# Second FFN input product in two passes over the features, and two of its conditioning units folded there

## The chip, the cores and the metric

The kernel runs on one core of one Trainium2 chip. The metric is the device time in microseconds (us) of one execution, from loading the inputs in HBM to having the output there.

## The reference, cut to what matters

A trunk of two layers over 256 tokens and 2048 features, in float32. Layer 0 mixes by pooling, layer 1 by an HGRN2 recurrence; each is followed by a SwiGLU FFN with 5632 hidden features. Six vectors for each layer (shift, scale and gate of the mixer and of the FFN) come from a conditioning vector.

```python
cond = jax.nn.silu(c)
for layer in range(DEPTH):
    mod = cond @ w_ada[layer] + b_ada[layer]            # 2048 -> 6 * 2048
    sh_m, sc_m, g_m, sh_f, sc_f, g_f = jnp.split(mod[:, None, :], N_MOD, axis=-1)
    h = rms_norm(x, norm_mix_gain[layer]) * (1.0 + sc_m) + sh_m
    y = pool_mixer(...) if layer == 0 else hgrn2_mixer(h, w_in, w_out, ...)
    x = x + g_m * y
    h = rms_norm(x, norm_ffn_gain[layer]) * (1.0 + sc_f) + sh_f
    a, b = jnp.split(h @ w_ffn_in[layer], 2, axis=-1)   # 2048 -> 2 * 5632
    x = x + g_f * ((jax.nn.silu(a) * b) @ w_ffn_out[layer])
return rms_norm(x, final_gain)
```

## The kernel before

**Products.** Every weight matrix is cut into chunks of 512 output columns, and a chunk into steps of 128 input features. A step is six matmuls on TensorE: for each of the two blocks of 128 tokens, high part by high part, high part by low part of the weight, low part of the feature by high part of the weight (L472 to L474), all added up in one of two PSUM buffers `prod`. A chunk with the whole 2048 features has 16 steps. There are 1392 steps in all, numbered through by the counter `step` that each engine keeps for itself; `START` gives the first step of each chunk. The stages, with the name of their first step: pooling (16 steps), first FFN input product (A0, 352 steps), first FFN output product (OUT0, 176), HGRN input product and recurrence (H0, 256), HGRN output product (W0, 64), second FFN input product (IN1, 352), second FFN output product (OUT1, 176). "H+75" below is the 75th step after H0.

**Weights.** Two steps are a pair. SyncE (SP) loads a pair to `raw`, ScalarE rounds it to `w_hi` (`hi`, L759), VectorE takes the rest to `w_lo` (`lo`, L1053), TensorE waits for `lo_ready` at every even step. There are four buffers (`SPL`), and ScalarE waits for `w_used` before it takes one again, so ScalarE and VectorE can be at most six steps ahead of TensorE.

**One order for each engine.** Each engine runs its instructions in the order in which they are written. The work between the products is hung by hand onto step numbers: `recurrence` on each engine does a piece of the HGRN recurrence at given steps after H0, once for each of four head groups of 64 steps. In a group TensorE turns forget and query values at 24 and 34, computes self scores at 37 and 38, eight levels of scores at 40, 45, ... 75 (in the last group at 40, 43, 46, 52, 55, 61, 64, 70, with turns of outputs between), and the output at 79 (74 in the last). VectorE does its part of a level in halves of a tile: exponents (L1394, L1395), decayed keys and queries (L1408, L1409), masked scores (L1429, L1436), five steps later in its own count (`LD`), since it is ahead.

**Conditioning units.** `mod` is computed in 24 units: one of the six vectors of a layer, one half of 1024 of its features. A unit is 16 tiles of `w_ada` of 128x1024. VectorE folds a tile into `acc` by one multiply-add (`fold`, L1088; the first tile of a unit by a multiply, L1085), then adds the bias by two instructions (L1097). `BEHIND` lists the units behind the head with the first and last step of their folds, which `due` spreads evenly. Three steps (`SUM`) behind the last, TensorE sums over partitions (`reduce_unit`): 16 small matmuls for shifts and scales (L516), four matmuls for gates (L537). ScalarE takes the result 8 steps later (`take_unit`). There is one `acc`: the first fold of a unit (L1085) waits for the sum of the unit before it. SP loads the tiles by the same step numbers into four buffers.

**First FFN input product.** For 9 of its 11 pairs of chunks (gate and value), `NA`, it runs in two passes over the features: first all 18 chunks over features 0 to 1023 (8 steps each), whose results ScalarE copies to `part_gate` and `part_value` in SBUF, then all over features 1024 to 2047; VectorE adds the stored halves (L1308, L1313), ScalarE applies SiLU in SBUF (L929). The last two pairs have 16 steps a chunk. Features 1024 to 2047 are normalised 118 steps after A0 (`FEATURES_B`), so their shift and scale units are folded inside the stage.

**Second FFN input product.** All 22 chunks have 16 steps over all features. The features are made by `features` at its start: groups 0 and 1 of 512 features ahead of the first matmuls, group 2 and 3 at steps 4 and 8. All four shift and scale units of this FFN, and the two gate units of HGRN, are folded between H+20 and W+32.

Of the kernel before, what the change touches and what calls it, by code (L numbers as in the profile page):

```python
# [14 lines left out]
CH = 512  # L15
# [24 lines left out]
def build(nc, x, c, norm_mix_gain, norm_ffn_gain, w_ada, b_ada, pool_w, pool_scale, hgrn_w_in,  # L40
# [38 lines left out]
    C_A = NCH  # L79
    C_B = C_A + 2 * NA  # L80
    C_OUT0 = C_B + 2 * NF
    C_H = C_OUT0 + NCH
    C_WOUT = C_H + 4 * NCH
    C_IN1 = C_WOUT + NCH
    C_OUT1 = C_IN1 + 2 * NF
# [7 lines left out]
    A0, B0, H0, W0, IN1, OUT1 = (START[n] for n in (C_A, C_B, C_H, C_WOUT, C_IN1, C_OUT1))  # L93
    OUT0 = START[C_OUT0]
    FEATURES_B = A0 + 118
# [33 lines left out]
    with ctx:  # L129
# [180 lines left out]
        def _(sp):  # L310
# [65 lines left out]
            for part in range(2):  # L376
                for j in range(NA):
                    for o in range(2):
                        load_chunk(w_ffn_in[0], o * F + j * CH, part * HALF, HALF, 0 if part or j or o else AHEAD)
            for j in range(NA, NF):  # L380
                for o in range(2):
                    load_chunk(w_ffn_in[0], o * F + j * CH, 0, KD)
# [15 lines left out]
            for j in range(NF):  # L398
                for o in range(2):
                    load_chunk(w_ffn_in[1], o * F + j * CH, 0, KD)  # L400
# [44 lines left out]
        def _(pe):  # L445
# [155 lines left out]
            def first_half(s):  # L601
                if s == 0:
                    turn_normalised()
                if s % 2 == 0:
                    t.tick("h")
                    pe.wait_ge(h_ready, t.get("h"))

            def second_features(_):
                if t.get("step") - 1 in (FEATURES_B + 2, FEATURES_B + 10):
                    turn_normalised()  # L610

            for c2 in range(2 * NA):
                h_product(second_features, None if c2 else first_half)

            def second_half(s):
                if s % 2 == 0:
                    t.tick("h")
                    pe.wait_ge(h_ready, t.get("h"))

            for j in range(NF):  # L620
                def turn_before(s):
                    if s == TURN:
                        if j <= NA:
                            pe.wait_ge(hidden_ready, j)
                            turn_tok()
                        else:
                            turn_hidden(C_B + 2 * j - 1)
                h_product(turn_before if j else None, None if j else second_half, HALF if j < NA else 0)
                h_product(None, None, HALF if j < NA else 0)
# [111 lines left out]
            for j in range(NF):  # L741
                def turn_in1(k):
                    if k == TURN:
                        turn_hidden(C_IN1 + 2 * j - 1)
                h_product(turn_in1 if j else None, None if j else features)
                h_product()
# [3 lines left out]
        def _(act):  # L750
# [137 lines left out]
            def first_half(k):  # L888
                if k == 0:
                    act.wait_ge(gain_ready, 3)  # L890
                    modulate(gain, mod[:, 1, 0:KD], 0)
                    modulate(gain, mod[:, 1, 0:KD], 1)

            def second_features():
                if t.get("step") == FEATURES_B + 8:
                    act.wait_ge(gain_ready, 4)
                    modulate(gain, mod[:, 1, 0:KD], 2)
                if t.get("step") == FEATURES_B + 16:
                    modulate(gain, mod[:, 1, 0:KD], 3)

            def part_of(chunk_at):
                j, o = (chunk_at - C_A) // 2, chunk_at % 2
                return (part_value if o else part_gate)[:, j]

            for c2 in range(2 * NA):
                def in_a(k):
                    if c2 == 0:
                        first_half(k)
                    second_features()
                    if c2 and k == EVAC:  # L910
                        take(C_A + c2 - 1, part_of(C_A + c2 - 1), ACT.Copy)
                chunk(in_a, AHEAD if c2 == 0 else 0)

# [5 lines left out]
            for j in range(NF):  # L919
                def in_gate(k):  # L920
                    if j == 0 and k == EVAC:
                        take(C_B - 1, part_of(C_B - 1), ACT.Copy)

                def in_value(k):
                    if j and k in (HID - HALF, HID - HALF + 1):
                        take_hidden(j - 1, k - HID + HALF)
                    if j < NA and k == EVAC:
                        evacuated(act, C_B + 2 * j)
                        act.activation(tok[:, :, :], tok[:, :, :], ACT.Silu).then_inc(silu_ready, 1)  # L929
                    if j >= NA and k == EVAC:  # L930
                        take(C_B + 2 * j, tok[:, :, :], ACT.Silu)
                chunk(in_gate)
                chunk(in_value)
# [97 lines left out]
            for j in range(NF):  # L1031
                def in_gate(k):
                    if j == 0:
                        features(k, gain, mod[:, 1, 0:KD], 6)
                    if j and k in (HID, HID + 1):
                        take_hidden(j - 1, k - HID)

                def in_value(k):
                    if k == EVAC:
                        take(C_IN1 + 2 * j, tok[:, :, :], ACT.Silu)  # L1040
                chunk(in_gate, 0 if j else AHEAD)
                chunk(in_value)
# [3 lines left out]
        def _(dve):  # L1046
# [238 lines left out]
            def in_a(_):  # L1285
                g = t.get("step")
                if g == FEATURES_B:
                    gains_of(C_GFFN, 1, HALF, HALF, UNIT[(0, SC_F, 1)])
                    normalise(2)
                if g == FEATURES_B + 8:  # L1290
                    normalise(3, 1)
                    split_feat(2)
                if g == FEATURES_B + 16:
                    split_feat(3)

            for c2 in range(2 * NA):
                def first_half(k):
                    if k == 0:
                        normalise(1, 1)
                        split_feat(0)  # L1300
                        split_feat(1)
                chunk(in_a, 0 if c2 else AHEAD, None if c2 else first_half)

            def add_gate(j):
                multiplied(dve, C_B + 2 * j)
                if j:
                    dve.wait_ge(small_full[1], t.get("small1"))
                dve.tensor_tensor(tok[:, :, :], prod[0][:, :, :], part_gate[:, j], ALU.add).then_inc(prod_free[0], 1)  # L1308

            def add_value(j):  # L1310
                multiplied(dve, C_B + 2 * j + 1)
                pv = part_value[:, j]
                dve.tensor_tensor(pv, prod[1][:, :, :], pv, ALU.add).then_inc(prod_free[1], 1)  # L1313
                dve.wait_ge(silu_ready, j + 1)
                evacuated(dve, C_B + 2 * j + 1)
                dve.tensor_tensor(tok[:, :, :], tok[:, :, :], pv, ALU.mult).then_inc(hidden_ready, 1)

# [13 lines left out]
            for j in range(NF):  # L1331
                def in_gate(k):
                    if j and k == LD - 1:
                        if j <= NA:
                            add_value(j - 1)
                        else:
                            take_value(C_B, j - 1)

                def in_value(k):
                    if j < NA and k == LD - 1:  # L1340
                        add_gate(j)
                    if j and k in (HID - HALF, HID - HALF + 1):
                        low_hidden(j - 1, k - HID + HALF)
                chunk(in_gate)
                chunk(in_value)

            def ffn_out(layer):
                base = C_OUT1 if layer else C_OUT0
                for n in range(NCH):
                    def in_out(k):  # L1350
                        if n == 0 and k == LD - 1:
                            take_value(C_IN1 if layer else C_B, NF - 1)
# [160 lines left out]
            for j in range(NF):  # L1513
                def in_gate(k):
                    if j and k == LD - 1:
                        take_value(C_IN1, j - 1)
                    if j and k in (HID, HID + 1):
                        low_hidden(j - 1, k - HID)
# [28 lines left out]
```

## Time and profile before

| what | value |
|---|---|
| median of 3 runs | 2308.41 us (2307.43 to 2310.44) |
| the profiled execution | 2310.61 us |
| its span, first to last instruction | 2308.6 us |
| TensorE busy | 2203.0 us, 95% |
| VectorE busy | 1622.6 us, 70% |
| ScalarE busy | 973.6 us, 42% |
| DMA engines, HBM rate | 74%, 248 GB/s |
| mean granted clock of TensorE | 0.977 |

TensorE is nearly always busy, so every microsecond that it waits between two matmuls is one of the time. The page gives shares over the whole span; the views below are by stage.

### The profile page before, as it was taken

The numbers are of one execution on the slowest core, as the hardware profiler recorded it, in microseconds if no ns is written. First come the engines' busy times: TensorE is split into PE (matmuls) and PEld (weight loads), VectorE is DVE, ScalarE is ACT, GpSimd is POOL, SyncE is SP. The second block draws the span as 40 slices with busy tenths as digits, with TensorE's granted clock in tenths as the row PEclk, the third lists the DMA queues.
The fourth block names the chain that finished last, engine by engine and source line by source line (L and its number), as shares of the span: only waits on it lengthen the run. The fifth ranks groups of instructions, "written<-read, shape, count | busy, mean of one in ns | idle before, by whom it ended". The sixth has DMA issues, their size and how long they took to land. (4 is left out here: it accounts for less than half of the span.)

```text
span 2308.6 us, 25674 instructions
## 1 busy us (share of the span) xinstructions
PE 2203.0 (95%) x10141; PEld 1835.7 (80%) x10141; DVE 1622.6 (70%) x1617; ACT 973.6 (42%) x1090; POOL 9.4 (0%) x43
## 2 busy tenths in 40 slices
PE   4887999999999999989999999989999999999997
PEld 4846888888888888878888887878888888888886
DVE  6788666788877667469899989955545457446644
ACT  2121444544444344455445445445444444444343
POOL 0000000000000000010000000000000000000000
PEclk9996899999999999999999999999999999999998
DMA  9988688878888888657777777755666678667764
GB/s 381 380 300 324 239 292 274 293 260 277 279 281 273 301 272 277 191 197 260 251 248 248 263 244 239 246 164 174 190 190 190 187 249 272 190 189 275 248 196 148
DMA packets 245895, 574.39 MB, mean 249 GB/s; under 512 B 17504, under 2 KB 17632, under 8 KB 245008
## 3 DMA queue, kind: packets, MB, share of 16 engines
q1 hardware_dynamic: 245776, 572.76, 74.1%
q8 instruction: 80, 1.31, 0.2%
q14 instruction: 39, 0.32, 0.0%
HBM read 570.59 MB, written 2.10 MB: 248 GB/s over the span
## 5 line engine op out<-in xcount | busy, mean ns | idle before, releaser
L1053 DVE TENSOR_TENSOR w_lo<-raw,w_hi 128x1024 fp32r<-128x1024 f32 x696 | 848.6, 1224 | 528.1 <-ACT w_hi L759 527.2
L759 ACT ACTIVATE w_hi<-raw 128x1024 fp32r<-128x1024 f32 x696 | 735.6, 1060 | 1021.4 <-PE prod L474 1018.9
L472 PE MATMUL prod<-w_hi,h_hi 128*128 128x512 f32 x2080 | 824.2, 396 | 0.3 <-DVE h_lo L1142 0.3
L474 PE MATMUL prod<-w_hi,h_lo 128*128 128x512 f32 x2080 | 812.8, 391 | 0.0
L473 PE MATMUL prod<-w_lo,h_hi 128*128 128x512 f32 x2080 | 812.3, 391 | 0.0
L474 PEld LDWEIGHTS prod<-w_hi,h_lo 128*128 128x128 f32 x2080 | 392.2, 189 | 83.2
L472 PEld LDWEIGHTS prod<-w_hi,h_hi 128*128 128x128 f32 x2080 | 392.8, 189 | 80.8 <-issue 1.2
L473 PEld LDWEIGHTS prod<-w_lo,h_hi 128*128 128x128 f32 x2080 | 392.8, 189 | 80.1 <-issue 1.4
L1088 DVE SCALAR_TENSOR_TENSOR acc<-ada,cond,acc 128x1024 f32<-128x1024 f32 x249 | 318.5, 1279 | 0.7
L472 PE MATMUL prod<-w_hi,g_hi 128*128 128x512 f32 x704 | 275.1, 391 | 0.0
L474 PE MATMUL prod<-w_hi,g_lo 128*128 128x512 f32 x704 | 273.9, 389 | 0.0
L473 PE MATMUL prod<-w_lo,g_hi 128*128 128x512 f32 x704 | 273.9, 389 | 0.0
L472 PEld LDWEIGHTS prod<-w_hi,g_hi 128*128 128x128 f32 x704 | 132.2, 188 | 27.9 <-issue 0.5
L473 PEld LDWEIGHTS prod<-w_lo,g_hi 128*128 128x128 f32 x704 | 132.2, 188 | 27.5 <-issue 0.5
L474 PEld LDWEIGHTS prod<-w_hi,g_lo 128*128 128x128 f32 x704 | 132.2, 188 | 27.5
L508 PE MATMUL modp<-cond,ada_head 128*128 128x1 f32 x384 | 82.8, 352 | 15.8 <-DMA ada_head<-in_w_ada 15.8
L508 PEld LDWEIGHTS modp<-cond,ada_head 128*128 128x128 f32 x384 | 82.6, 333 | 15.9 <-DMA ada_head<-in_w_ada 15.9
L546 PE MATMUL small<-ident,tok 128*128 128x128 f32 x304 | 48.5, 312 | 48.3 <-DVE tok L1135 30.0
L546 PEld LDWEIGHTS small<-ident,tok 128*128 128x128 f32 x304 | 41.3, 161 | 55.3 <-DVE tok L1135 35.1
L788 ACT ACTIVATE mod<-modp 128x8 f32<-128x8 f32 x16 | 2.8, 178 | 142.2 <-PE modp L516 142.2
L681 PEld LDWEIGHTS small<-qdec,kdec 128*128 128x128 f32 x448 | 53.5, 191 | 7.8 <-issue 6.3
L681 PE MATMUL small<-qdec,kdec 128*128 128x64 f32 x448 | 53.7, 273 | 3.0 <-DVE qdec L1409 3.0
(142 smaller groups left out, 1017.7 us busy)
## 6 DMA issues: line engine op xcount, KB each, us to landing
raw<-in_w_ffn_in SPq DMA_DIRECT2D x352, 512.0 KB, 4.1
ada<-in_w_ada SPq DMA_DIRECT2D x288, 512.0 KB, 5.4
raw<-in_w_ffn_out SPq DMA_DIRECT2D x176, 512.0 KB, 4.4
raw<-in_hgrn_w_in SPq DMA_DIRECT2D x128, 512.0 KB, 4.0
ada_head<-in_w_ada SPq DMA_DIRECT2D x96, 512.0 KB, 7.8
raw<-in_hgrn_w_out SPq DMA_DIRECT2D x32, 512.0 KB, 4.5
raw<-in_pool_w SPq DMA_DIRECT2D x8, 512.0 KB, 6.2
xs<-in_x SPq DMA_DIRECT2D x2, 1024.0 KB, 17.1
```

What stands on the lines that cost most here:

```text
L472: pe.matmul(o, hi[:, k, ts], wh, start=(begin and s == 0), stop=False)
L473: pe.matmul(o, hi[:, k, ts], wl, start=False, stop=False)
L474: mm = pe.matmul(o, lo[:, k, ts], wh, start=False, stop=(end and s == n - 1))
L508: mm = pe.matmul(modp[:, 0, j:j + 1], ada_buffer(slot)[:, j * P:(j + 1) * P], cond[:, k:k + 1], start=False, stop=(last and k == KD - 1 an ...
L546: mm = pe.transpose(small[half][:, o:o + P], block_of(tb, 2 * half + j), ident[:, :])
L681: mm = pe.matmul(small[b][:, o:o + H], kdec[:, b, hd, blk * P:(blk + 1) * P], qdec[:, b, hd, blk * H:(blk + 1) * H], start=True, stop=True)
L759: act.activation(w_hi[:, slot], raw[:, r], ACT.Copy).then_inc(hi_ready, 1)
L788: act.activation(mod[:, 0 if section < SH_F else 1, at:at + UB], modp[:, 0, 0:UB], ACT.Copy).then_inc(unit_taken, 1)
L1053: dve.tensor_tensor(w_lo[:, slot], raw[:, r], w_hi[:, slot], ALU.subtract).then_inc(lo_ready, 1)
L1088: ins = dve.scalar_tensor_tensor(a, ada_buffer(slot), cond[:, k:k + 1], a, ALU.mult, ALU.add)
```

## The change

Two things. The second FFN input product gets the structure of the first: 18 half chunks over features 0 to 1023, 18 over 1024 to 2047, 4 whole chunks, with the same code for both layers (`ffn_in(layer)` on each engine, `load_ffn_in(layer)` on SP). Features 1024 to 2047 are then normalised 118 steps after its start (A1), and only the first half of the gains is wanted ahead of it. And the unit list: the second halves of shift and scale (`(1, SH_F, 1)`, `(1, SC_F, 1)`) are folded at A1+2 to A1+50 and A1+56 to A1+106, as in layer 0. The four units that stay in HGRN get 48 steps each (H+24, H+82, H+140, H+200), and none is folded after H+248.

```diff
-    STEPS = [HG] * NCH + [HALF] * (4 * NA) + [KD] * (2 * (NF - NA)) + [KF] * NCH + [KD] * (5 * NCH + 2 * NF) + [KF] * NCH
+    FFN_IN = [HALF] * (4 * NA) + [KD] * (2 * (NF - NA))
+    STEPS = [HG] * NCH + FFN_IN + [KF] * NCH + [KD] * (5 * NCH) + FFN_IN + [KF] * NCH
...
-    FEATURES_B = A0 + 118
+    FEATURES_B = (A0 + 118, A1 + 118)
...
-              ((1, SH_F, 0), H0 + 20, H0 + 62, None), ((1, SH_F, 1), H0 + 68, H0 + 110, None),
-              ((1, SC_F, 0), H0 + 116, H0 + 158, None), ((1, SC_F, 1), H0 + 164, H0 + 204, None),
-              ((1, G_M, 0), H0 + 210, H0 + 246, None), ((1, G_M, 1), H0 + 254, W0 + 32, W0 + 47),
+              ((1, SH_F, 0), H0 + 24, H0 + 72, None), ((1, SC_F, 0), H0 + 82, H0 + 130, None),
+              ((1, G_M, 0), H0 + 140, H0 + 188, None), ((1, G_M, 1), H0 + 200, H0 + 248, W0 + 47),
+              ((1, SH_F, 1), A1 + 2, A1 + 50, None), ((1, SC_F, 1), A1 + 56, A1 + 106, A1 + 116),
               ((1, G_F, 0), OUT1 - 116, OUT1 - 60, None), ((1, G_F, 1), OUT1 + 46, OUT1 + 84, OUT1 + 110)]
...
             update(C_WOUT + NCH - 1, NCH - 1, gate[:, 1], UNIT[(1, G_M, 1)])
-            norm_prepare(C_GFFN + KD, 1, UNIT[(1, SC_F, 1)])
-
-            for j in range(NF):
-                def in_gate(k):
-                    if j and k == LD - 1:
-                        take_value(C_IN1, j - 1)
-                    if j and k in (HID, HID + 1):
-                        low_hidden(j - 1, k - HID)
-                chunk(in_gate, 0 if j else AHEAD, None if j else features)
-                chunk()
+            gains_of(C_GFFN + KD, 1, 0, HALF, UNIT[(1, SC_F, 0)])
+            norm_root()
+            ffn_in(1)
             ffn_out(1)
```

VectorE's part of the two passes, as it now runs for both layers:

```diff
+            def ffn_in(layer):
+                base_b, second = C_B[layer], FEATURES_B[layer]
+
+                def in_a(_):
+                    g = t.get("step")
+                    if g == second:
+                        gains_of(C_GFFN + layer * KD, 1, HALF, HALF, UNIT[(layer, SC_F, 1)])
+                        normalise(2)
+                    if g == second + 8:
+                        normalise(3, 1)
+                        split_feat(2)
+                    if g == second + 16:
+                        split_feat(3)
+
+                def first_half(k):
+                    if k == 0:
+                        if layer:
+                            normalise(0)
+                        normalise(1, 1)
+                        split_feat(0)
+                        split_feat(1)
...
+                def add_gate(j):
+                    multiplied(dve, base_b + 2 * j)
...
+                    dve.tensor_tensor(tok[:, :, :], prod[0][:, :, :], part_gate[:, j], ALU.add).then_inc(prod_free[0], 1)
+
+                def add_value(j):
+                    multiplied(dve, base_b + 2 * j + 1)
+                    pv = part_value[:, j]
+                    dve.tensor_tensor(pv, prod[1][:, :, :], pv, ALU.add).then_inc(prod_free[1], 1)
+                    dve.wait_ge(silu_ready, layer * NA + j + 1)
+                    evacuated(dve, base_b + 2 * j + 1)
+                    dve.tensor_tensor(tok[:, :, :], tok[:, :, :], pv, ALU.mult).then_inc(hidden_ready, 1)
```

## Rows read from the trace of the kernel before

**Rows 1.** Stages: start:end, length, busy time (x instructions) of each engine, clock, DMA.
```profile
core 0: us, PE busy (x) PEld busy (x) DVE busy (x) ACT busy (x) POOL busy (x), PEclk, DMA share, GB/s
241.60:742.10 500.50, 500.50 (x2279) 415.61 (x2278) 384.62 (x351) 232.61 (x244) 0.00 (x0) 1.00 0.82 281
...
998.80:1449.80 451.00, 442.27 (x2287) 374.36 (x2286) 406.47 (x478) 230.15 (x247) 0.00 (x0) 0.99 0.75 250
1449.80:1559.40 109.60, 101.22 (x477) 83.43 (x476) 83.04 (x92) 51.30 (x70) 0.00 (x0) 0.97 0.64 202
1559.40:2052.50 493.10, 493.10 (x2215) 408.44 (x2214) 268.14 (x242) 214.42 (x222) 0.00 (x0) 1.00 0.67 205
```

**Rows 2.** Waits of the whole span: engine, line, releaser: total us, times, longest.
```profile
PE small L676 <- DVE sdiag L1414: 5.3, 2, 3.8
...
PE small L681 <- DVE qdec L1409: 3.0, 5, 0.8
...
PE small L655 <- DVE smask L1429: 1.6, 2, 1.2
...
PE prod L472 <- DVE h_lo L1142: 0.3, 1, 0.3
```

**Rows 3.** Timeline of TensorE from H+65: start, length, line, xcount.
```profile
1103.78 0.39 PE L472 MATMUL prod<-w_hi,h_hi 128*128 128x512 f32 x1
...
1104.46 1.89 PE L681 MATMUL small<-qdec,kdec 128*128 128x64 f32 x16
...
1106.19 1.90 PE L516 MATMUL modp<-ones,acc 128*128 128x1 f32 x16
...
1107.95 0.49 PE L472 MATMUL prod<-w_hi,h_hi 128*128 128x512 f32 x1
...
1112.39 0.40 PE L472 MATMUL prod<-w_hi,h_hi 128*128 128x512 f32 x1
```

**Rows 4.** Timeline of TensorE at H+203 and H+232, idle time before in brackets.
```profile
1347.61 0.39 PE L472 MATMUL prod<-w_hi,h_hi 128*128 128x512 f32 x1
...
1349.26 1.97 PE L681 MATMUL small<-qdec,kdec 128*128 128x64 f32 x16 [0.81 <-DVE qdec L1409]
...
1398.09 0.39 PE L472 MATMUL prod<-w_hi,h_hi 128*128 128x512 f32 x1
...
1402.71 2.08 PE L676 MATMUL small<-qdec,kdec 128*128 128x128 f32 x8 [3.78 <-DVE sdiag L1414]
```

**Rows 5.** The table of stages for two short stretches, for the granted clock.
```profile
1402.30:1405.70 3.40, 2.99 (x11) 2.80 (x12) 3.40 (x5) 0.00 (x0) 0.00 (x0) 0.50 0.75 220
1108.80:1112.20 3.40, 3.40 (x10) 2.63 (x9) 3.40 (x5) 0.95 (x1) 0.00 (x0) 0.51 0.26 51
```

**Rows 6.** Waits of VectorE from H0 to the end of W, total us, times, longest.
```profile
DVE acc L1085 <- PE modp L516: 21.9, 4, 8.5
```

**Rows 7.** Timeline of VectorE: three first folds of a unit, at A0+56, H+116, H+210.
```profile
318.67 0.75 DVE L1085 TENSOR_SCALAR acc<-ada,cond 128x1024 f32<-128x1024 f32 x1 [4.74 <-PE modp L516]
...
1190.44 0.75 DVE L1085 TENSOR_SCALAR acc<-ada,cond 128x1024 f32<-128x1024 f32 x1 [4.57 <-PE modp L516]
...
1361.17 0.75 DVE L1085 TENSOR_SCALAR acc<-ada,cond 128x1024 f32<-128x1024 f32 x1 [8.46 <-PE modp L516]
```

**Rows 8.** Timeline of VectorE among the levels, where it waits for nothing.
```profile
1294.86 1.28 DVE L1088 SCALAR_TENSOR_TENSOR acc<-ada,cond,acc 128x1024 f32<-128x1024 f32 x1
1296.05 1.23 DVE L1053 TENSOR_TENSOR w_lo<-raw,w_hi 128x1024 fp32r<-128x1024 f32 x1
1297.19 0.69 DVE L1394 TENSOR_TENSOR dec<-bT 128x512 f32<-128x512 f32 x1
...
1298.39 1.29 DVE L1088 SCALAR_TENSOR_TENSOR acc<-ada,cond,acc 128x1024 f32<-128x1024 f32 x1
```

**Rows 9.** Groups of instructions by line: busy us, mean ns, idle before.
```profile
L1308 DVE TENSOR_TENSOR tok<-prod,part_gate 128x1024 f32<-128x1024 f32 x9 | 11.0, 1225 | 9.2 <-PE prod L474 9.2
...
L841 ACT ACTIVATE part_gate<-prod 128x1024 f32<-128x1024 f32 x9 | 9.1, 1013 | 0.0
```

**Rows 10.** Timeline at the first matmul of the second FFN input product.
```profile
1559.42 0.78 PE L472 MATMUL prod<-w_hi,h_hi 128*128 128x512 f32 x1
...
1559.81 0.88 DVE L1135 TENSOR_SCALAR tok<-xs,rstd 128x512 f32<-128x512 f32 x2
```

More of the change, by code:

```diff
@@ L375, in _, with load_ffn_in @@
             load_unit(10, KD)
-            for part in range(2):
-                for j in range(NA):
+            def load_ffn_in(layer):
+                for part in range(2):
+                    for j in range(NA):
+                        for o in range(2):
+                            load_chunk(w_ffn_in[layer], o * F + j * CH, part * HALF, HALF, 0 if layer or part or j or o else AHEAD)
+                for j in range(NA, NF):
                     for o in range(2):
[L379 to L382, printed above, removed]
+                        load_chunk(w_ffn_in[layer], o * F + j * CH, 0, KD)
+            load_ffn_in(0)
             for n in range(NCH):
@@ L397, in _ @@
                 load_chunk(hgrn_w_out[0], n * CH, 0, KD)
-            for j in range(NF):
-                for o in range(2):
-                    load_chunk(w_ffn_in[1], o * F + j * CH, 0, KD)
+            load_ffn_in(1)
             for n in range(NCH):
@@ L599, in _ @@
             head_unit(7)
[L601 to L629, printed above, removed]
+            def ffn_in(layer):
+                def first_half(s):
+                    if s == 0:
+                        turn_normalised()
+                        if layer:
+                            turn_normalised()
+                    if s % 2 == 0:
+                        t.tick("h")
+                        pe.wait_ge(h_ready, t.get("h"))
+                def second_features(_):
+                    if t.get("step") - 1 in (FEATURES_B[layer] + 2, FEATURES_B[layer] + 10):
+                        turn_normalised()
+                def second_half(s):
+                    if s % 2 == 0:
+                        t.tick("h")
+                        pe.wait_ge(h_ready, t.get("h"))
+                for c2 in range(2 * NA):
+                    h_product(second_features, None if c2 else first_half)
+                for j in range(NF):
+                    def turn_before(s):
+                        if s == TURN:
+                            if j <= NA:
+                                pe.wait_ge(hidden_ready, layer * NA + j)
+                                turn_tok()
+                            else:
+                                turn_hidden(C_B[layer] + 2 * j - 1)
+                    h_product(turn_before if j else None, None if j else second_half, HALF if j < NA else 0)
+                    h_product(None, None, HALF if j < NA else 0)
@@ L739, in _ @@
                 h_product()
[L741 to L746, printed above, removed]
+            ffn_in(1)
             ffn_out(C_OUT1)
@@ L886, in _ @@
             take_unit(7)
[L888 to L912, printed above, removed]
             def take_hidden(j, half):
@@ L917, in take_hidden, with ffn_in, part_of, in_a @@
                                small[half][:, :].rearrange("p (a s) -> p a s", a=2), ACT.Copy).then_inc(ghi_ready, 1)
-            for j in range(NF):
-                def in_gate(k):
[L921 to L933, printed above, removed]
+            def ffn_in(layer):
+                base_a, base_b, second = C_A[layer], C_B[layer], FEATURES_B[layer]
+                shifts = mod[:, 1, 0:KD]
+                def part_of(chunk_at):
+                    j, o = (chunk_at - base_a) // 2, chunk_at % 2
+                    return (part_value if o else part_gate)[:, j]
+                for c2 in range(2 * NA):
+                    def in_a(k):
+                        if c2 == 0 and k == 0:
+                            act.wait_ge(gain_ready, 6 if layer else 3)
+                            modulate(gain, shifts, 0)
+                            modulate(gain, shifts, 1)
+                        if t.get("step") == second + 8:
+                            act.wait_ge(gain_ready, 7 if layer else 4)
+                            modulate(gain, shifts, 2)
+                        if t.get("step") == second + 16:
+                            modulate(gain, shifts, 3)
+                        if c2 and k == EVAC:
+                            take(base_a + c2 - 1, part_of(base_a + c2 - 1), ACT.Copy)
+                    chunk(in_a, AHEAD if c2 == 0 else 0)
+                for j in range(NF):
+                    def in_gate(k):
+                        if j == 0 and k == EVAC:
+                            take(base_b - 1, part_of(base_b - 1), ACT.Copy)
+                    def in_value(k):
+                        if j and k in (HID - HALF, HID - HALF + 1):
+                            take_hidden(j - 1, k - HID + HALF)
+                        if j < NA and k == EVAC:
+                            evacuated(act, base_b + 2 * j)
+                            act.activation(tok[:, :, :], tok[:, :, :], ACT.Silu).then_inc(silu_ready, 1)
+                        if j >= NA and k == EVAC:
+                            take(base_b + 2 * j, tok[:, :, :], ACT.Silu)
+                    chunk(in_gate)
+                    chunk(in_value)
@@ L1029, in _ @@
             root()
[L1031 to L1034, printed above, removed]
-                    if j and k in (HID, HID + 1):
[L1036 to L1042, printed above, removed]
+            ffn_in(1)
             ffn_out(1)
@@ L1283, in _ @@
             gains_of(C_GFFN, 1, 0, HALF, 7)
[L1285 to L1316, printed above, removed]
             def take_value(base, j):
```

57 lines of the change are left out of this document (33 added, 24 removed).

## The prediction, made before the changed kernel had run

> **What bounds the kernel now.** I read the table of stages first. TensorE is busy through the whole of both FFN input products (500.50 of 500.50 us, 493.10 of 493.10) and lacks 8.7 us in HGRN and 8.4 in its output product [rows 1]. So the FFN stages are at TensorE's pace, and only idle time of TensorE can be won. Second I read TensorE's waits. Those that the change touches are all on VectorE, in HGRN and its output product: 5.3 us in 2 waits of level 0 for the masked self scores, 3.0 in 5 waits of levels for the decayed queries, 1.6 in 2 turns of outputs for a masked score, 0.3 for split features; 10 waits, 10.2 us [rows 2]. Third comes VectorE's own state there. It is busy 406.47 of 451.00 us, 90% [rows 1], but of the rest 21.9 us is four waits of L1085, the first fold of a unit, for TensorE's sum of the unit before [rows 6]: one lasts 4.57 us at H+116, one 8.46 us at H+210 [rows 7]. VectorE stands still there with all that is written behind L1085, and then has to catch up while TensorE comes closer. The reader is to see both: the folds take VectorE's time, and they block it.
>
> **The pace.** Three matmuls take 0.68 us (1103.78 to 1104.46), a step 1.36, a level's 16 small matmuls 1.73, a unit's column sum 1.76 (1106.19 to 1107.95) [rows 3].
>
> **What the waits are worth.** The bracket of an idle time is counted from a modelled end. Start to start, a level comes 0.68 us after the last L472 of its step when nothing is late [rows 3]. At H+203 it comes 1.65 later, so 0.97 is lost where the bracket says 0.81; at H+232 it is 4.62, so 3.94 against 3.78 [rows 4]. Each wait costs 0.16 more than its bracket: 10.2 + 10 x 0.16 = 11.8 us. Behind the long wait the granted clock is at 0.50 (1.2 GHz) for 3.4 us [rows 5]. The price of such a stretch can be read at H+66, where the same drop follows a level and a column sum in one step: 1107.95 to 1112.39 is 4.44 us for four times 0.68, 1.7 lost, of which 0.1 is usual behind small matmuls; 1.6 us [rows 3, 5].
>
> **Part 1: the units.** Two units leave HGRN: 32 folds and four bias adds. A fold takes 1.19 us of VectorE from its start to the next one's, a `lo` 1.14, a half 0.60 [rows 8]; so some 38 us of VectorE go to the next stage. Column sums move with them, 2 x 1.76 = 3.5 us of TensorE out of HGRN and 3.5 into A1, nothing in the sum. The gate sum of W moves into H, nothing in the sum.
> The blocks: a unit now starts 10, 10 and 12 steps behind the last step of the one before it, and its sum stands 3 steps behind that. VectorE is at most 6 ahead, so when it gets there TensorE is past the sum: the 21.9 us of blocking go. Before, the distance was 6 steps.
> Wait by wait. H+232 (3.94): VectorE starts the unit at H+210 at 1361.17 after 8.46 blocked, and the masked self scores are due at its step H+236. After the change nothing blocks there and 13 folds fall between H+200 and H+236 instead of 12; 8.46 - 1.2 = 7.3 us earlier, up to its lead of 6 steps (8.2 us). The wait goes, and with it its clock drop. H+114 and H+119 (0.8 each): block of 4.57 at H+116, same number of folds; they go. H+168 (1.7): a block of the same kind at H+164, one fold more; it goes. H+193 and H+203: 8 folds instead of 13 between H+164 and there; they go. H+75: the block at H+68 is replaced by 2 folds (2.4 us); it goes. The turns at H+241 and H+259 and the split at H+279 stand behind folds and bias adds that are no longer there: with the new list the last fold is at H+245. All ten go: 11.8 us, and one clock drop, 1.6.
> The other drop stays, I think. Its cause, a level and a column sum in one step (H+65), comes back at H+75, where the sum of the first unit again meets a level.
> Is VectorE fast enough with the new spacing? Five steps with a level take TensorE 5 x 1.36 + 1.73 = 8.5 us. VectorE has 2.5 `lo` (2.85), six halves (3.6) and folds every 3.06 steps (1.63 x 1.19 = 1.9): 8.4. Before, at one fold in 2.6 steps, it was 8.7, and 9.0 at the 2.3 steps of H+210: above TensorE's pace. So it now holds its lead, narrowly.
>
> **Part 2: the two passes.** TensorE has the same steps. Added in SBUF and PSUM traffic: 18 copies on ScalarE at 1.01 us (18.2) and 18 adds on VectorE at 1.22 (22.0) [rows 9]; with the folds VectorE comes to some 268 + 43 + 22 = 333 us in 497. Layer 0 has the same stage with three units more and is busy 384.62 of 500.50, with no idle time of TensorE [rows 1]. Even L1085 blocks there, 4.74 us at A0+56 [rows 7], the distance that A1 gets, and it costs TensorE nothing. Priced at nothing. The cover is the 6 steps of lead and the second `prod` buffer; without them the 18 copies would cost 18.2. The check on this: 493.1 + 4 x 1.76 = 500.1 for the four more column sums of layer 0, against 500.5 measured.
> The start of the stage: two multiplies of group 2 (0.88 us) no longer stand ahead of the second split. They run at 1559.81, after the first matmul at 1559.42 [rows 10], so they are not on the path; the first fold at A1+2 takes their place. Nothing, with bounds of -0.9 and +0.9. The half-clock stretch at this start depends on where the wait falls, between -1.6 and +1.6 by the price above. SP issues the same weight tiles in halves of the features, and the 32 tiles of `w_ada` move behind fewer of them; layer 0 runs at 281 GB/s with this mix [rows 1].
> The page "TensorE: Matmul & The Clock Gate" of the Trainium skill, section "What's actually happening", calls the gate's window free-running, so that the same kernel can have a longer or shorter slow stretch. By it neither drop in HGRN need come where I put it, and the sum could be 1.6 us either way.
>
> **The sum.** 11.8 + 1.6 = 13.4 us. The profiled execution would be 2308.6 - 13.4 = 2295.2 us of span and 2310.61 - 13.4 = 2297.2 in time; it lies 2.2 above the median of the runs. From the median: 2308.4 - 13.4 = 2295.0 us. Its own range is 2290.5 to 2298.5: the other clock drop gone and the start of the stage 1.6 better at one end, 2 us of waits left and the start worse at the other.
>
> **The rivals.**
> A, part of it: the balance 8.4 against 8.5 is too narrow, since VectorE has self scores, scan, forget and output besides, and new waits come at other levels. For it: the closeness; against it: the free stretches of 10 steps between units, and the blocks that are gone. Half of the 13.4 stays: 2301.7 us.
> B, no change: the waits are the latency of the loop TensorE, VectorE, ScalarE and back, not a backlog. VectorE's block and its folds are then no matter, and the unit list only moves them: 2308. Against it: most levels of the same form have no wait, and each wait stands behind a block or a dense unit.
> C, slower: the copies of half chunks are on the path. The place is `take` at step 7 of each following half chunk of 8 steps (10.9 us); TensorE wants that buffer again at its end. From the point where ScalarE has lost its lead of 6 steps, every copy stops TensorE: 18 x 1.01 = 18.2 more, less the 13.4, 2313.2 us. Against it: 232.61 us of 500.50 on ScalarE in layer 0, and no idle TensorE [rows 1].
> The page "TensorEngine Tiling (Array Packing)" of the Trainium skill, section "PSUM Bottleneck", warns that evacuation does not get faster with the matmuls and may become the limit; two passes double what is evacuated, so it speaks for C, and the trace of layer 0 does not bear it out.
>
> **How the numbers follow.** Forecast 0.72, A 0.14, B 0.07, C 0.07. A measurement of this kernel can tell some 0.2% (4.6 us) from no change. Faster by more: forecast and nearly all of A, 0.85; within: B and a little of A, 0.08; slower: C, 0.07. The range leaves out B and C and reaches to A with a microsecond for the spread of the runs: 2290.5 to 2302.5 us.
>
> **What the profile would show.** Right: TensorE's waits on L1414, L1409 and L1429 nearly gone; L1085 in HGRN waiting under 2 us; HGRN at 451.0 - 10.0 - 1.6 - 3.5 + 1.7 = 437.6 us (the 1.7 is the gate sum, at the price of a column sum), its output product near 106, the second FFN input product near 496.6 with TensorE without idle time. Wrong: waits for L1409 between H+90 and H+130 or at H+168 (A), waits as before with VectorE idle (B), an input product over 500 us with waits on L841 (C).

## The result, and the profile after

The changed kernel takes 2295.89 us (median of 5 runs, 2295.14 to 2298.19), the kernel before 2310.27 us (median of 5, 2307.43 to 2310.54). The medians lie 14.4 us apart. The ratio over all the runs is 0.9943, 95% interval 0.9932 to 0.9953, which is 13.2 us of 2310. Forecast were 2295.0 us and a gain of 13.4. A second series of both kernels gave 0.9942 (0.9929 to 0.9954).

The table of stages of the changed kernel: from the first step of each stage to that of the next, its length, the busy time of each engine, clock and DMA. It answers to [rows 1].

```profile
core 0: us, PE busy (x) PEld busy (x) DVE busy (x) ACT busy (x) POOL busy (x), PEclk, DMA share, GB/s
239.60:740.50 500.90, 500.90 (x2279) 415.89 (x2278) 384.58 (x351) 232.55 (x244) 0.00 (x0) 1.00 0.81 281
...
997.10:1435.50 438.40, 437.20 (x2258) 371.14 (x2257) 388.04 (x460) 229.91 (x245) 0.00 (x0) 0.99 0.71 231
1435.50:1541.50 106.00, 99.14 (x474) 82.94 (x472) 64.20 (x73) 51.20 (x71) 0.00 (x0) 0.96 0.55 178
1541.50:2038.00 496.50, 496.50 (x2246) 411.79 (x2245) 327.44 (x297) 232.07 (x242) 0.00 (x0) 1.00 0.72 233
```

The reader is to see three differences. HGRN goes from 451.0 to 438.4 us, its output product from 109.6 to 106.0, and the second FFN input product grows from 493.1 to 496.5, where TensorE is still busy to the last hundredth. Together 12.8 us less. The rest of the difference between the two profiled executions (14.5 us of span) lies ahead of HGRN, which begins 1.7 us earlier here (A0 2.0 earlier). It is not the change's, for the second profiled execution of the changed kernel, shown below, has its HGRN stage begin at 998.8 as before.

What TensorE still waits for in the recurrence, from H0 to the end of the output product, against [rows 2]:

```profile
PE small L689 <- DVE qdec L1408: 1.2, 2, 0.7
```

Of ten waits of TensorE with 10.2 us, two are left with 1.2, and both are new ones. The waits of VectorE's first folds for a column sum (21.9 us in four, now L1076) are gone from the list of this stretch altogether. Both fit the argument.

The end of the third unit, on VectorE and then on TensorE, at H+183:

```profile
1300.38 1.28 DVE L1079 SCALAR_TENSOR_TENSOR acc<-ada,cond,acc 128x1024 f32<-128x1024 f32 x1
1301.69 1.39 DVE L1088 TENSOR_TENSOR acc<-acc,bias 1x512 f32<-1x512 f32 x2
...
1305.69 1.97 PE L689 MATMUL small<-qdec,kdec 128*128 128x64 f32 x16 [0.55 <-DVE qdec L1408]
```

The last fold of a unit is followed at once by its two bias adds: 2.7 us of VectorE from 1300.38 to 1303.12, among levels where it has no such time, and the decayed queries of the level come late. The wait at H+247 (0.65 us) comes later behind the end of the fourth unit: its two bias adds end at 1408.9, and VectorE works without a pause from there to the queries at 1417.43, with two splits of features on its way.

And the clock drop at H+75, against [rows 3] and [rows 5]:

```profile
1120.09 1.89 PE L689 MATMUL small<-qdec,kdec 128*128 128x64 f32 x16
...
1121.82 1.90 PE L520 MATMUL modp<-ones,acc 128*128 128x1 f32 x16
...
1123.58 0.49 PE L476 MATMUL prod<-w_hi,h_hi 128*128 128x512 f32 x1
...
1128.02 0.39 PE L476 MATMUL prod<-w_hi,h_hi 128*128 128x512 f32 x1
```

A level and a column sum in one step, and behind them 4.44 us for four times 0.68, as at H+66 before. The granted clock between 1124.6 and 1127.9 is 0.50.

### The profile page after: what moved, and what is told of

Read it like the earlier page. It is cut to its first block and busy times, and to the rows that moved or that the text cites. A ratio compares the mean times of both kernels' runs of the same rounds, so it can differ in the third digit from the quotient of the medians.

```text
span 2294.1 us, 25736 instructions
## 1 busy us (share of the span) xinstructions
PE 2198.6 (96%) x10141; PEld 1835.1 (80%) x10141; DVE 1644.5 (72%) x1636; ACT 990.7 (43%) x1108; POOL 9.4 (0%) x43
```

## The experiments

Theory: what TensorE loses in HGRN, it loses by VectorE, in two ways, the folds' load among the levels and the block at the first fold of a unit; the unit list removes both, and the two passes cost and give nothing by themselves, they only make room for two units. Rivals: the two passes themselves give or cost something; the waits are the latency of the loop between the engines (rival B).

### The two passes alone

```diff
-              ((1, SH_F, 0), H0 + 24, H0 + 72, None), ((1, SC_F, 0), H0 + 82, H0 + 130, None),
-              ((1, G_M, 0), H0 + 140, H0 + 188, None), ((1, G_M, 1), H0 + 200, H0 + 248, W0 + 47),
-              ((1, SH_F, 1), A1 + 2, A1 + 50, None), ((1, SC_F, 1), A1 + 56, A1 + 106, A1 + 116),
+              ((1, SH_F, 0), H0 + 20, H0 + 62, None), ((1, SH_F, 1), H0 + 68, H0 + 110, None),
+              ((1, SC_F, 0), H0 + 116, H0 + 158, None), ((1, SC_F, 1), H0 + 164, H0 + 204, None),
+              ((1, G_M, 0), H0 + 210, H0 + 246, None), ((1, G_M, 1), H0 + 254, W0 + 32, W0 + 47),
```

> The changed kernel with the unit list of the kernel before: two passes in the second FFN input product, all six units folded between H+20 and W+32. Theory (the unit list carries the whole gain, the two passes are worth nothing): HGRN near 451 us, its output product near 109.6, TensorE's waits on VectorE there near 10 us in 10 waits, the second FFN input product near 493 us with TensorE never idle; ratio to the kernel before 0.999 to 1.001. Rival C (copies of half chunks cost time): the input product over 495 us, ratio up to 1.008. Rival (the two passes give something at their start): the input product under 491.5 us.

Measured: ratio 0.9999 (0.9990 to 1.0008). HGRN, its output product and the second FFN input product:

```profile
997.20:1448.20 451.00, 442.45 (x2287) 374.49 (x2286) 406.40 (x478) 230.23 (x247) 0.00 (x0) 0.99 0.75 250
1448.20:1557.90 109.70, 101.33 (x478) 83.50 (x476) 83.12 (x93) 51.35 (x71) 0.00 (x0) 0.97 0.63 202
1557.90:2051.00 493.10, 493.10 (x2214) 408.39 (x2213) 288.04 (x261) 231.94 (x240) 0.00 (x0) 1.00 0.67 205
```

These three stages have their length of before to a tenth, with 20 us more on VectorE and 17.5 more on ScalarE in the last one, and the waits are back (5.3, 3.0, 1.4 and 0.3 us). To within the interval of 0.1% the passes neither give nor take; the whole gain goes by the unit list. The 3.4 us by which the input product grew are the two column sums.

### The copies doubled

```diff
                         if c2 and k == EVAC:
+                            if layer:
+                                multiplied(act, base_a + c2 - 1)
+                                act.activation(part_of(base_a + c2 - 1), prod[(base_a + c2 - 1) % 2][:, :, :], ACT.Copy).then_inc(copied, 1)
+                                act.wait_ge(copied, c2)
                             take(base_a + c2 - 1, part_of(base_a + c2 - 1), ACT.Copy)
```

> The changed kernel with each of the 18 copies of a half chunk in layer 1 done twice, the second waiting for the first: 18 times 1.0 to 1.2 us more on ScalarE. Theory (the copies lie under six steps of lead and a second buffer): no time, second FFN input product 496.5 us, TensorE never idle there. Rival C (they are at the edge of the path): up to 18 to 22 us more.

Measured: ratio 0.9941 (0.9926 to 0.9956). 17 of the 18 fall in this edit (the last one is taken elsewhere). The second FFN input product:

```profile
1543.10:2039.50 496.40, 496.40 (x2247) 411.64 (x2246) 327.48 (x297) 248.11 (x259) 0.00 (x0) 1.00 0.72 233
```

16 us more on ScalarE and not a tenth in the stage, where the changed kernel's second execution has 496.40 too. Rival C is out: not even twice the copies cost TensorE anything.

### The blocks taken away, the load kept

The kernel before with the same six units in the same stretch, each packed tighter, so that ten steps lie between them.

```diff
-              ((1, SH_F, 0), H0 + 20, H0 + 62, None), ((1, SH_F, 1), H0 + 68, H0 + 110, None),
-              ((1, SC_F, 0), H0 + 116, H0 + 158, None), ((1, SC_F, 1), H0 + 164, H0 + 204, None),
-              ((1, G_M, 0), H0 + 210, H0 + 246, None), ((1, G_M, 1), H0 + 254, W0 + 32, W0 + 47),
+              ((1, SH_F, 0), H0 + 20, H0 + 56, None), ((1, SH_F, 1), H0 + 66, H0 + 102, None),
+              ((1, SC_F, 0), H0 + 112, H0 + 148, None), ((1, SC_F, 1), H0 + 158, H0 + 194, None),
+              ((1, G_M, 0), H0 + 204, H0 + 240, None), ((1, G_M, 1), H0 + 250, W0 + 30, W0 + 47),
```

> The kernel before with the same six units in the same stretch (H+20 to W+30), but 10 steps between a unit's last and the next one's first instead of 6, and so 37 steps a unit, a fold each 2.3 steps. Theory of the block (VectorE standing still at the first fold of a unit makes most of the loss): VectorE waits under 3 us at the first folds instead of 21.9, the 3.8 us wait at H+232 is gone, 6 to 9 us faster, ratio 0.996 to 0.9975. Theory of the load (the folds among the levels are too many): VectorE needs 9.0 us for each 8.5 us of TensorE among the levels, so more waits for L1409 than before, together over 10 us, ratio 1.000 or more.

Measured: ratio 0.9971 (0.9960 to 0.9983). The two stages, and TensorE's waits for VectorE's recurrence in them:

```profile
997.00:1442.00 445.00, 439.15 (x2287) 372.03 (x2286) 409.56 (x480) 230.45 (x247) 0.00 (x0) 1.00 0.77 255
1442.00:1550.60 108.60, 101.16 (x477) 83.47 (x476) 81.02 (x90) 51.18 (x70) 0.00 (x0) 0.97 0.62 198
```

```profile
PE small L681 <- DVE qdec L1409: 3.6, 6, 1.1
PE small L676 <- DVE sdiag L1414: 2.2, 2, 1.3
...
PE small L655 <- DVE og L1458: 0.3, 1, 0.3
PE small L655 <- DVE smask L1429: 0.3, 1, 0.3
```

553.6 us for the two stages against 560.6 before: 7.0 us by new places for the same units, without moving one of them out. No first fold waits for a sum any more, the wait of 3.8 us at H+232 is down to 1.3, and both clock drops are gone. The 7.0 us are 3.8 us less of waits and the two drops at 1.6 each. Only one of these drops stood behind a wait. The other, at H+66, stood behind a column sum in the step of a level, and it went because the first unit now ends at H+56 and its sum, at H+59, meets no level. So some 5.4 us are the blocks' and 1.6 are the place of that sum. And 6.4 us of waits stay, most of them at other levels, with a fold in 2.3 steps. The blocks are thus not the whole; what the load does by itself, the next run shows.

### The load taken away, the blocks kept

The kernel before with its folds in HGRN done on one column of 1024. The other 1023 columns are left out, so its results are not the reference's; a fold takes VectorE 0.2 us and all waits, sums and transfers stay.

```diff
                 a = unit_buffer(u)
+                width = 1 if 16 <= u <= 21 else UW
...
-                    ins = dve.scalar_tensor_tensor(a, ada_buffer(slot), cond[:, k:k + 1], a, ALU.mult, ALU.add)
+                    ins = dve.scalar_tensor_tensor(a[:, 0:width], ada_buffer(slot)[:, 0:width], cond[:, k:k + 1], a[:, 0:width], ALU.mult, ALU.add)
```

> The kernel before with the folds of all six units in HGRN done on one of 1024 columns (their values are not the reference's): the load of the folds goes, the blocks stay, VectorE still waits for the sums at L1085. Theory (a block costs TensorE only where VectorE has no slack to catch up): L1085 waits 20 us or more, TensorE waits under 2 us for VectorE, HGRN 439 to 442 us. Rival (the blocks alone make the waits): the waits at H+114, H+168 and H+232 stay, 4 to 8 us together.

Measured in one execution: HGRN 438.7 us, a little under the expected 439 to 442. Its stage, and VectorE's waits at the first folds (now L1086) for column sums and a gate sum:

```profile
998.70:1437.40 438.70, 438.61 (x2286) 373.93 (x2285) 329.44 (x480) 229.29 (x247) 0.00 (x0) 0.99 0.77 257
```

```profile
DVE acc L1086 <- PE modp L516: 22.7, 4, 7.9
...
DVE acc L1086 <- PE modp L537: 2.6, 1, 2.6
```

VectorE stands still for 25.3 us and TensorE's list has no wait for the recurrence. At these places a block alone costs next to nothing; with the load behind it, it costs time. So the two parts do not add up to the gain: taking away the load removes all 10.2 us of waits, taking away the blocks, with folds a little denser, 3.8 of them. What is lost arises where both meet. The drop behind H+65 is still there in this run, as it should be by its cause, and the one at H+232 went with its wait.

The same edit on the changed kernel (units 16 to 19), where there are no blocks:

> The changed kernel with the folds of the four units in HGRN done on one of their 1024 columns (the shift, scale and gate values are then not the reference's): VectorE's time for folds goes, every wait, sum and transfer stays. Theory (the two waits left, 0.8 us each at H+183 and H+247, come from the end of a unit, a fold and two bias adds in a row): both vanish, HGRN at 436.7 us, and the clock drop behind H+75 stays. Rival B (what is left is latency of the loop between the engines): the two waits stay and HGRN stays at 438.4.

Measured in one execution: HGRN 436.5 us, no wait for the recurrence, the clock drop behind H+75 still there. The bias adds stay in this run (1.39 us at 1301.90), so by themselves they make no wait; it takes the folds ahead of them. What is left above 436.5 in the changed kernel, 1.9 us, goes with the folds.

### The blocks put back into the changed kernel, twice

First with six steps between the units:

```diff
-              ((1, SH_F, 0), H0 + 24, H0 + 72, None), ((1, SC_F, 0), H0 + 82, H0 + 130, None),
-              ((1, G_M, 0), H0 + 140, H0 + 188, None), ((1, G_M, 1), H0 + 200, H0 + 248, W0 + 47),
+              ((1, SH_F, 0), H0 + 24, H0 + 72, None), ((1, SC_F, 0), H0 + 78, H0 + 126, None),
+              ((1, G_M, 0), H0 + 132, H0 + 180, None), ((1, G_M, 1), H0 + 186, H0 + 234, W0 + 47),
```

> The changed kernel with its four units in HGRN 6 steps apart instead of 10 to 12 (H+24, H+78, H+132, H+186), 48 steps each as before. Theory of the block: VectorE waits again at the first folds, 10 to 17 us in three waits, and TensorE waits 3 to 6 us for it, 1.5 to 4 us slower than the changed kernel. Theory of the load: as the changed kernel, HGRN 438 to 439 us, since a fold still comes each 3 steps and only two are among 64 steps more.

Measured: ratio 0.9966 (0.9954 to 0.9978); HGRN is 5.2 us longer than in the changed kernel, more than the 1.5 to 4 expected. VectorE waits 16.5 us in three blocks, as expected, but TensorE's waits are only 1.8 us (changed kernel 1.2), not 3 to 6. What makes HGRN 443.6 us long are slow stretches at half clock, three instead of one:

```profile
1125.70:1129.10 3.40, 3.40 (x10) 2.65 (x9) 3.40 (x4) 0.00 (x0) 0.00 (x0) 0.50 0.25 42
1217.90:1224.70 6.80, 6.80 (x19) 5.54 (x20) 5.80 (x7) 1.65 (x3) 0.00 (x0) 0.50 0.26 77
1323.70:1327.10 3.40, 3.40 (x10) 2.61 (x9) 3.37 (x5) 1.26 (x2) 0.00 (x0) 0.50 0.88 301
```

10.2 us more at half clock are some 4.8 us by the price of [rows 3]. The first two stand right behind H+75 and H+129, where a level and a column sum share a step. The third stands behind the level at H+188, which had waited 1.3 us. The next run has the same six steps with no sum in the step of a level:

```diff
+              ((1, SH_F, 0), H0 + 22, H0 + 70, None), ((1, SC_F, 0), H0 + 76, H0 + 124, None),
+              ((1, G_M, 0), H0 + 130, H0 + 178, None), ((1, G_M, 1), H0 + 184, H0 + 234, W0 + 47),
```

> The changed kernel with its four units in HGRN 6 steps apart again, but placed so that no column sum stands in the step of a level (sums at H+73, H+127, H+181, H+237 against levels at H+75, H+129, H+183, H+238). The run with six steps between had 1.8 us of waits for VectorE but was 5.2 us longer in HGRN, with three half-clock stretches more than the changed kernel. Theory (the sums in the steps of levels make the stretches, the blocks only the waits): no half-clock stretch in HGRN, waits of 1.5 to 2.5 us, HGRN 437 to 438 us. Rival (the blocks cost it, in another form): HGRN 441 us or more.

Measured: ratio 0.9985 (0.9975 to 0.9994), HGRN 448.8 us. The theory fell, and further than its rival had it. TensorE's waits in HGRN are

```profile
PE small L689 <- DVE qdec L1408: 7.1, 6, 1.9
```

and there are again three slow stretches, 13.6 us. The start of the stage was faster in this execution than in the changed kernel's, with the level at H+60 95.5 us after H0 where it is 97.1 there, so the 448.8 us understate the loss by 1.6. Around H+183, first VectorE, then TensorE:

```profile
1310.68 0.75 DVE L1076 TENSOR_SCALAR acc<-ada,cond 128x1024 f32<-128x1024 f32 x1 [6.62 <-PE modp L541]
1311.35 0.68 DVE L1428 TENSOR_TENSOR smask<-small,masks 128x512 f32<-128x512 f32 x1
1312.07 0.69 DVE L1435 TENSOR_TENSOR sdiag<-sdiag,smask 128x512 f32<-128x512 f32 x1
1312.68 1.22 DVE L1044 TENSOR_TENSOR w_lo<-raw,w_hi 128x1024 fp32r<-128x1024 f32 x1
1313.82 0.68 DVE L1407 TENSOR_TENSOR kdec<-kT,dec 128x512 f32<-128x512 f32 x1
1314.42 0.69 DVE L1408 TENSOR_TENSOR qdec<-qT,dec 128x512 f32<-128x512 f32 x1
```

```profile
1308.77 1.88 PE L541 MATMUL modp<-acc,ones 128*128 128x512 f32 x4
...
1315.25 3.14 PE L689 MATMUL small<-qdec,kdec 128*128 128x64 f32 x16 [1.88 <-DVE qdec L1408]
```

TensorE does the sum at H+181 and wants the level at H+183, two steps later. VectorE, freed by the sum at 1310.68, has six instructions to do before the queries of that level are there, until 1315.11. Two steps last 2.7 us. In the run with the sums at H+75, H+129, H+183, each sum stood behind the level of its step, and five steps lay until the next one or none followed in that group. So, by these two runs, the price of a block is not its length; it is set by the work that VectorE has between the release and the next thing that TensorE needs, against the steps between the two. And a wait beside a level can bring the slow clock too: the stretches here begin at 1124.7, 1220.2 and 1315.8, each at a level that had waited, 1.72, 1.72 and 1.88 us. The length of the wait does not settle it: 1.29 us at H+188 of the run before this one brought a stretch, 1.52 us at H+168 of the kernel before brought none. What does settle it, no run here shows.

### The drop at H+75 and the two waits

The first unit two steps earlier (H+22 to H+70), nothing else:

> The changed kernel with its first unit in HGRN two steps earlier (H+22 to H+70), so that its column sum stands at H+73 and not in the step of a level. Theory (the slow stretch comes from 32 small matmuls in a row in one step): no half-clock stretch between H+60 and H+90, HGRN 1.6 us shorter, near 436.8. Rival (the place of the slow stretch follows its own count and not this step): a stretch of 3.4 us at half clock is still somewhere in HGRN, its length unchanged at 438.4.

Measured on one chip: the changed kernel 2296.09 us (2292.89 to 2298.00, ratio 0.9942), this one 2297.07 (2294.99 to 2297.66, ratio 0.9945, 0.9933 to 0.9958): no difference that can be told. In the profiles:

```profile
998.80:1437.00 438.20, 436.96 (x2259) 370.89 (x2258) 388.04 (x460) 229.97 (x245) 0.00 (x0) 0.99 0.70 231
```

```profile
999.00:1436.40 437.40, 435.64 (x2258) 369.68 (x2257) 388.40 (x460) 229.85 (x245) 0.00 (x0) 1.00 0.70 231
```

The first is the changed kernel, the second this one. The clock's share goes to 1.00 and no half-clock stretch is left in HGRN behind its start, so the rival, that the stretch would come at another place, is out here. But only 0.8 us of the 1.6 show: a third wait came up at H+65 (waits 1.8 us in 3), behind a fold that now stands ahead of that level. Two steps trade a drop for a wait.

The unit list spread further, with the gate units at 3.5 and 4.7 steps a fold and the last one running into the output product:

```diff
+              ((1, SH_F, 0), H0 + 22, H0 + 70, None), ((1, SC_F, 0), H0 + 82, H0 + 130, None),
+              ((1, G_M, 0), H0 + 142, H0 + 198, None), ((1, G_M, 1), H0 + 210, W0 + 20, W0 + 47),
```

> The changed kernel with the unit list spread further: first unit at H+22 to H+70, third at H+142 to H+198, fourth at H+210 to W+20, so that folds end later and are 3.5 and 4.7 steps apart. Theory: the waits of 0.8 and 0.9 us at H+183 and H+247 and the slow stretch go, 3.3 us less in HGRN than the changed kernel, 435.1 us; ratio to the kernel before 0.9925 to 0.993. Rival: new waits in the output product, where folds now run beside updates of x (before the change 1.3 and 0.5 us at H+259 and H+279).

Measured: 2292.48 us (2292.13 to 2295.28), ratio 0.9931 (0.9918 to 0.9943); HGRN and output product 434.7 + 107.7 = 542.4 us against 438.2 + 105.9 = 544.1. Half of the expected 3.3 for the two stages together. HGRN alone is shorter than the expected 435.1, but 1.8 us of that went into the output product, where the gate sum of the last unit now stands. The waits at H+183 and H+247 are gone, two of 0.5 and 0.4 us are left at H+65 and H+232. With those two places moved as well:

```diff
+              ((1, SH_F, 0), H0 + 24, H0 + 74, None), ((1, SC_F, 0), H0 + 84, H0 + 132, None),
+              ((1, G_M, 0), H0 + 142, H0 + 198, None), ((1, G_M, 1), H0 + 208, W0 + 20, W0 + 47),
```

> The run with the spread unit list, with its first unit at H+24 to H+74 (sum at H+77), the second at H+84 to H+132, the fourth from H+208: the waits of 0.8 at H+65 and 0.7 at H+232 that it still had should go. Theory: HGRN with output product 541.0 us against 542.4 there and 544.1 in the changed kernel, no half-clock stretch in HGRN; ratio to the kernel before 0.992 to 0.9935. Rival: waits of the same size turn up at other levels, 542.4 or more.

Measured: 2292.15 us (2292.10 to 2293.86), ratio 0.9928 (0.9916 to 0.9941).

```profile
997.10:1430.20 433.10, 433.10 (x2254) 369.23 (x2253) 380.74 (x452) 229.89 (x245) 0.00 (x0) 1.00 0.71 231
1430.20:1538.00 107.80, 100.94 (x478) 83.73 (x477) 71.69 (x82) 51.25 (x71) 0.00 (x0) 0.96 0.57 186
```

540.9 us, expected 541.0. TensorE is busy through all of HGRN, 433.10 of 433.10. It is the fastest of all lists tried; its lead over the changed kernel is 3.2 us in the stages and within the overlap of the two intervals in time.

The runs beside each other, in us (waits as the view counts them, from H0 to the end of the output product; the blocks are those for column sums and for gate sums, 21.9 and 1.5 in the kernel before). The kernels with all six units have two column sums more in HGRN and one gate sum less, 1.8 us together that are no loss:

| kernel | folds among the levels | blocks of VectorE | TensorE's waits for the recurrence | half clock in HGRN behind its start | HGRN |
|---|---|---|---|---|---|
| before | one in 2.2 to 2.7 steps | 23.4 | 10.2 | 6.8 | 451.0 |
| before, ten apart | one in 2.3 | none | 6.4 | 0 | 445.0 |
| before, thin folds | next to no load | 25.3 | none | 3.4 | 438.7 |
| changed | one in 3.1 | none | 1.2 | 3.4 | 438.4 |
| changed, six apart | one in 3.1 | 16.5 | 1.8 | 13.6 | 443.6 |
| changed, six apart, off levels | one in 3.1 | 19.7 | 7.1 | 13.6 | 448.8 |
| changed, thin folds | next to no load | none | none | 3.4 | 436.5 |

## Why the prediction was right

**What bounds the kernel** held: what was won is TensorE's idle time in HGRN and its output product, all of it behind VectorE, and one clock drop. The FFN stages gave nothing.

**The sum** was 13.4 us: ten waits, 11.8, and one clock drop, 1.6. All ten went, and the drop went with the longest. Against it came two new waits at H+183 and H+247, 1.2 us by the view and 1.5 with the 0.16 that each costs more, which I had priced at nothing. The stages show 12.8 us where 13.4 - 1.5 = 11.9 would be left. The other 0.9 us are not shown one by one. Waits too short for the view's brackets fit them: in the kernel before the levels at H+60 and H+65 come 8.73 and 8.71 us behind the level ahead of them, where 8.63 is usual, and the changed kernel has 8.63 there. So the total came out within 0.6 us of the forecast with two errors of opposite sign; that closeness is luck. The low end of the forecast's own range, 2290.5, is not what its terms give either: 2295.0 less two times 1.6 is 2291.8. Nothing hung on it.

**The balance of 8.4 against 8.5** (the step of rival A) was the weak one, as feared. It counts folds and levels only. The bias adds at a unit's end, 1.4 us, and the scan, self scores and output splits are not in it, and both new waits stand where one or two of these fall among levels. Rival A was right in kind and had its size wrong: 1.5 us, not 6.7.

**The blocks.** That all 21.9 us of them would go was right. But the prediction gave five of the ten waits (H+75, H+114, H+119, H+168, H+232; 7.1 us by the view) to the block in front of each, and that overstated the block. With the blocks gone and folds a little denser, 2.4 us are left at these five places, and others come up, 6.4 us in all. With the load gone and the blocks kept, none is left. With light load, blocks at six steps' distance bring 0.6 us of waits more or 5.9, by where the sum stands before the next level, and slow stretches besides. New places for the units brought 7.0 us; the rest of the gain took the lower load, which the prediction names as the other half of the cause but prices at no wait of these five. The places of before were of the middling sort, with a sum one step before the level at H+113, and VectorE too loaded to make up.

**Rival B** (latency) is out by the two runs with thin folds: the loop between the engines is the same and no wait is left. **Rival C** is out by the doubled copies.

**Two passes at nothing** held, 496.5 us against 496.6 forecast for the stage; so did HGRN at 438.4 against 437.6 and the output product at 106.0 against 106.

**The drop at H+75** stood where it was put, in both profiled executions of the changed kernel and in every run that kept this sum; the chance that it would come elsewhere, 1.6 us either way, did not come about. The cause given, a level and a sum in one step, is borne out by the run that moved the sum by two steps and by the kernel before with its units ten apart, but it is not the only one: waits beside levels can bring it as well.

## What to carry to other kernels

A hand-placed background job on an engine that runs its instructions in order can hurt in two ways that feed each other: its load takes the slack, and its own waits, which stop everything written behind it, then have nothing to be made up from. In this kernel the waits were harmless without the load, and with the load kept, 6.4 of the 10.2 us stayed without them. Look at the engine's idle time as well as at its busy time: here it was 90% busy and still spent 23 us waiting for a result that a few steps' more distance would have had ready; new places alone were worth 7 us without moving any work, some 5.4 of them by the distance. When such a wait can't be avoided, put it where the other engine needs nothing for as long as it takes to work off what has queued up, and mind the last step of the job, where more falls at once.

## What the runs showed of the hardware

TensorE's clock fell to its lower level (0.50, 1.2 GHz) with no recorded idle time ahead of it, behind 32 small matmuls in a row (1120.09 to 1123.58), in the kernel before, in the changed one and in every other run here whose first column sum shares its step with a level; moving the sum by two steps left HGRN at 1.00. A row of small matmuls is not enough by itself: at H+207 of the kernel before, 24 matmuls of 128 columns and the 16 of a column sum follow each other from 1356.61 to 1360.99, and the granted clock stays at 1.00 there and behind them. The Trainium skill, "TensorE: Matmul & The Clock Gate", section "What's actually happening", gives idleness as what lowers the clock. The row shows no idle time, but it cannot settle the point: the ends of matmuls are modelled, and a matmul of one column takes as long from start to start (1.76 us for 16) as one of 64 (1.73), so the array may well stand idle inside the row. Whether it does, no run here shows.
